# Second mixer of an encoder layer: the two parts of a tile's sums are added before the turn, on GpSimd

## The chip, the cores and the metric

One core of one Trainium2 chip. The metric is the device time of one execution, in microseconds (us), of a kernel that computes one whole encoder layer for 2048 tokens. Engines are named as the profile names them: PE is TensorE, DVE is VectorE, ACT is ScalarE, POOL is GpSimd, SP is SyncE, which here issues the DMAs.

## The reference, cut to what matters

The layer has an input projection, two attention mixers side by side, an output projection, an MLP and a gated extra input. The change is in mixer B only: eight heads of 64 columns, three dilated window patterns over the same keys, a relative-position bias, and a softmax merged over the patterns by its denominators.

```python
def dilated_pattern(q, k, v, rel_bias, window, dilation):
    ...
    sc = jnp.einsum('brnqhd,brnkhd->brnqhk', qs, ks) * (HEAD_DIM ** -0.5)
    sc = jnp.where(valid, sc + bias, NEG_BIG)
    mx = jnp.max(sc, axis=-1)
    e = jnp.exp(sc - mx[..., None])
    den = jnp.sum(e, axis=-1)
    o = jnp.einsum('brnqhk,brnkhd->brnqhd', e, vs) / den[..., None]
    ...
def mixer_b(q, k, v, rel_bias):
    ...
    y = (w[0][..., None] * outs[0] + w[1][..., None] * outs[1] + w[2][..., None] * outs[2]) / w_sum[..., None]
```

For a query tile this comes to: scores, bias, one maximum, one exponential with its sum, the product with the values, and a division by the sum of exponentials.

## The kernel before, in words

The program runs four stages one after the other: the input projection, mixer A, mixer B (`mixer_b_phase`), and the feed stage with everything after the mixers. Mixer B lasts from about 1228 to 1650 us of the span.

Mixer B has 8 heads of 16 query tiles of 128 tokens. Every engine runs the same nest: a hardware loop of four turns, two heads written out in each (`par`), and in each head 16 tiles `n` written out. `N` is the tile's number over all heads. A tile has seven or eight blocks of 128 keys: seven where `n % 4` is 0 or 3 (an edge tile, `first_tile`), eight else (a full tile). All operands of matmuls are split in a high part and a low part, to keep float32's precision with a faster matmul format: queries, keys and values by GpSimd one head ahead, the exponentials inside the tile by ScalarE (high) and VectorE (low).

A tile goes through these steps. TensorE `scores` (L1292, L1300) writes a score tile; VectorE `add_bias` (L1441, three parts) adds the bias and takes maxima, then the row's maximum (L1444). ScalarE `exponential` (L1374) works in SBUF and sums. TensorE `turn` (L1311) transposes seven or eight blocks into two PSUM banks; ScalarE `turned_hi` (L1381, one copy a bank) and VectorE `turned_lo` (L1451) write the high and the low part `pT`. TensorE `values` (L1323) multiplies by the values: stationary are the values' high and low part side by side (64 + 64 columns), moving are both parts of `pT` (256 columns), so that the result `out_acc` holds 128 rows (value part, column) by 256 columns (part of the exponential, query). ScalarE `sums_out` (L1387) copies it to `oT`. TensorE `fold_out` (L1331) transposes both 128-column halves of `oT` back into `out_acc`. VectorE `output` (L1463) multiplies 256 columns by the reciprocal of the sum (`rden`, from `sums_of_two`, L1458) into `y_part`. GpSimd `summed` adds, for two tiles at once, first the two halves of the exponential's parts (L1250) and then the two parts of the values (L1255) into the staging buffer `y_st`, which SyncE stores four tiles at a time (`store`, L1145).

The order on each engine is written out by hand, and each engine takes its instructions strictly in that order. In step `N`:

- TensorE: `scores(N + 2)`, `turn(N + 1)`, `fold_out` of tile `N - 1`, `values(N)`. `values(N)` waits until `output` of tile `N - 2` has freed the accumulator.
- ScalarE: `turned_hi(N + 1)` (two copies), `exponential(N + 2)`, `sums_out(N)`.
- VectorE: `add_bias(N + 2)`, `output` of tile `N - 1`, in even tiles `sums_of_two`, `turned_lo(N + 1)`.
- GpSimd, per head, in long pieces: the last sums of the head before, then eight pieces of the next head's queries and keys (`split_pre`, L1228 with L1232 or L1235, 512 columns each), with `summed` after every second; then all of the next head's values at once (`split_values`, L1240 and L1242, 2048 elements a row), `summed`, then twenty copies of bias tables (`tables`, L1201 to L1214), and two more `summed`.
- SyncE, per head: the stores of chunk 0 and 1, `load_next` (key and query loads, L89, once the split of the head before it in these buffers is done; then the values, one transfer L94 and 24 small ones L102, once `split_values` is done), then the stores of chunk 2 and 3, then the bias tables (L109, L115).

The staging buffer has two halves, so the first `summed` of a head (tiles 0 and 1) waits until the store of the previous head's chunk 2 has landed, and the third until that of chunk 3 has.

```python
def one(h, par, nxt):
    store(h, 0)
    store(h, 1)
    load_next(h + 1, nxt)
    store(h, 2)
    store(h, 3)
    next_tables(h + 1, 1 - par, nxt)
```

## Time and profile before

| what | us |
|---|---|
| median of 3 runs | 3468.54 (3468.3 to 3469.4) |
| the profiled execution, its own time | 3470.07 |
| its span | 3468.3 |
| TensorE busy over the span | 3341.7 |
| VectorE busy | 2360.2 |
| ScalarE busy | 1853.6 |
| GpSimd busy | 1863.4 |
| mean granted clock of TensorE | 0.987 of full |

The profile is of one execution. Its span begins with the first and ends with the last instruction; the execution's own time, 1.8 us longer, holds what lies around it. Busy times are per engine and overlap. A row of the timeline gives the start of a group of neighbouring instructions, its length, engine, line, operation, output<-inputs, shape and count; a bracket behind it gives idle time just before and what ended it. Ends of matmuls are modelled, so starts are the safer reading. "SPq" rows are DMA issues on SyncE's queue; the time of a transfer itself, from issue to landing, stands in the groups of DMAs.

### The profile page before, as it was taken

The page shows a single profiled execution, that of the slowest core. Times are in us where ns is not written, and L with a number is a line of the kernel's source. Part 1 is how long each engine was busy: PE and PEld are TensorE (multiplying, and loading weights), DVE is VectorE, ACT ScalarE, POOL GpSimd, SP SyncE. Part 2 cuts the span into 40 slices and gives each one's busy share as a digit, 9 for nine tenths or more (in the row PEclk, how much of TensorE's full clock was granted, in tenths as well). Part 3 has the DMA queues.
Part 4 walks back from the last instruction along what each step waited for, and adds up shares of the span by engine and source line. Part 5 has one row for each costly group of instructions (what it writes and reads, how often), then busy time and mean ns, then how long its engine had stood idle before and what let it go on. Part 6 is the DMA issues. An engine that isn't in the chain of part 4 may idle for free.

```text
span 3468.3 us, 54646 instructions
## 1 busy us (share of the span) xinstructions
PE 3341.7 (96%) x17366; PEld 2799.6 (81%) x17366; DVE 2360.2 (68%) x4253; ACT 1853.6 (53%) x3489; POOL 1863.4 (54%) x1365
## 2 busy tenths in 40 slices
PE   8999989999999979999799999999999999999997
PEld 6878878888888868888588888888888888888886
DVE  5556679999898989999455574555655556555554
ACT  3222268888888867777434454343544435443333
POOL 5555534445442257667177750777506776067770
PEclk9999999999999989999899999999999999999998
DMA  5455444444442234343444447444474444744443
GB/s 186 159 181 166 143 133 142 147 161 161 153 153 69 47 86 95 83 105 94 165 128 154 150 159 248 158 152 149 154 267 141 151 154 144 256 160 144 144 136 137
DMA packets 234386, 512.87 MB, mean 148 GB/s; under 512 B 113780, under 2 KB 132668, under 8 KB 214364
## 3 DMA queue, kind: packets, MB, share of 16 engines
q1 hardware_dynamic: 224860, 496.91, 44.4%
q10 hardware_dynamic: 9344, 13.73, 1.1%
q8 instruction: 90, 1.47, 0.2%
q14 instruction: 92, 0.75, 0.1%
HBM read 427.43 MB, written 95.58 MB: 151 GB/s over the span
## 4 chain that ended last, share of the span: by engine, by line
PE 47%; DVE 2%; DMA 1%; ACT 1%; issue 1%; POOL 0%; SPq 0%; DVEq 0%
PE feed_bank L1771 45%; PE feed_bank L1854 1%; PE feed_bank L1762 1%; PE feed_bank L1881 1%; ACT feed_xT L1973 0%; DMA feed_w_split<-scr_wG 0%; DMA feed_comb<-scr_wG 0%; POOL feed_w_split L1727 0%; DMA feed_y_in<-scr_yB 0%; DVE feed_xT L2129 0%; DVE feed_sums L2265 0%; DVE feed_total L2219 0%; ACT feed_w_split L2025 0%; DVE feed_total L2144 0%; DVE feed_ms L2108 0%
## 5 line engine op out<-in xcount | busy, mean ns | idle before, releaser
L1727 POOL TENSOR_TENSOR feed_w_split<-feed_w_raw,feed_w_split 128x1024 fp32r<-128x1024 f32 x352 | 882.0, 2515 | 249.6 <-ACT feed_w_split L2025 236.2
L1771 PE MATMUL feed_bank<-feed_w_split,feed_comb 128*128 128x512 f32 x3552 | 822.1, 391 | 16.6 <-DVE feed_sums L2265 7.8
L1771 PEld LDWEIGHTS feed_bank<-feed_w_split,feed_comb 128*128 128x128 f32 x3552 | 664.6, 188 | 162.5 <-POOL feed_w_split L1727 11.6
L1771 PE MATMUL feed_bank<-feed_xT,feed_w_split 128*128 128x512 f32 x3072 | 701.8, 390 | 2.6 <-DVE feed_xT L2129 2.6
L1771 PEld LDWEIGHTS feed_bank<-feed_xT,feed_w_split 128*128 128x128 f32 x3072 | 578.4, 188 | 123.6 <-DVE feed_xT L2129 3.0
L1052 DVE TENSOR_TENSOR mixa_pT<-mixa_turned,mixa_pT 128x512 fp32r<-128x512 f32 x512 | 350.8, 685 | 62.1 <-ACT mixa_pT L994 52.6
L1724 POOL TENSOR_SCALAR feed_w_split<-feed_w_raw 128x1024 fp32r<-128x1024 f32 x128 | 136.5, 1066 | 464.3 <-PE feed_bank L1771 190.1
L994 ACT ACTIVATE mixa_pT<-mixa_turned 128x512 fp32r<-128x512 f32 x512 | 306.7, 599 | 122.6 <-PE mixa_turned L930 103.1
L875 PE MATMUL mixa_out_acc<-mixa_pT,mixa_v_hl 128*128 128x512 f32 x1028 | 365.1, 437 | 0.7 <-DVE mixa_pT L1052 0.7
L2219 DVE TENSOR_TENSOR feed_total<-feed_total,feed_bank 128x512 f32<-128x512 f32 x352 | 224.4, 681 | 195.8 <-PE feed_bank L1771 192.9
L2040 ACT ACTIVATE feed_rl<-feed_bank 128x512 f32<-128x512 f32 x128 | 76.5, 598 | 524.4 <-PE feed_bank L1771 524.4
L2025 ACT ACTIVATE feed_w_split<-feed_w_raw 128x1024 fp32r<-128x1024 f32 x224 | 236.0, 1062 | 189.3 <-PE feed_bank L1771 185.5
L1019 DVE TENSOR_REDUCE mixa_nmax<-mixa_score 128x1 f32<-128x1024 f32 x264 | 322.4, 1221 | 8.4 <-PE mixa_score L862 1.3
L930 PE MATMUL mixa_turned<-layer_ident,mixa_prob 128*128 128x128 f32 x2048 | 306.7, 272 | 0.0
L930 PEld LDWEIGHTS mixa_turned<-layer_ident,mixa_prob 128*128 128x128 f32 x2048 | 252.4, 141 | 55.6
L964 ACT ACTIVATE mixa_prob<-mixa_score,mixa_nmax 128x1024 f32<-128x1024 f32 x263 | 294.3, 1119 | 2.8 <-DVE mixa_nmax L1019 2.8
L862 PE MATMUL mixa_score<-mixa_kT,mixa_qT 128*128 128x512 f32 x1056 | 288.4, 395 | 2.4 <-ACT mixa_prob L964 2.2
L2188 DVE TENSOR_TENSOR feed_comb<-feed_rl,feed_comb 128x256 fp32r<-128x256 f32 x128 | 154.4, 1207 | 175.1 <-ACT feed_comb L2044 174.8
L862 PEld LDWEIGHTS mixa_score<-mixa_kT,mixa_qT 128*128 128x128 f32 x1056 | 198.0, 188 | 50.6 <-ACT mixa_prob L964 4.0
L386 PE MATMUL proj_bank<-proj_w_split,proj_xT 128*128 128x512 f32 (+1 forms) x768 | 180.5, 355 | 0.0
L1381 ACT ACTIVATE mixb_pT<-mixb_turned 128x512 fp32r<-128x512 f32 (+1 forms) x258 | 137.3, 570 | 68.9 <-PE mixb_turned L1311 68.9
L339 POOL TENSOR_SCALAR proj_w_split<-proj_w_raw 128x2048 fp32r<-128x2048 f32 x36 | 73.3, 2036 | 185.9 <-ACT proj_st L453 63.7
(204 smaller groups left out, 5563.1 us busy)
## 6 DMA issues: line engine op xcount, KB each, us to landing
feed_w_raw<-scr_wT SPq DMA_DIRECT2D x160, 512.0 KB, 3.3
feed_w_split<-scr_wG SPq DMA_DIRECT2D x68, 1024.0 KB, 5.0
feed_w_raw<-w_tail_dram SPq DMA_DIRECT2D x128, 512.0 KB, 3.5
proj_w_raw<-w_in_dram SPq DMA_DIRECT2D x39, 1024.0 KB, 5.3
feed_w_raw<-w_ff_dram SPq DMA_DIRECT2D x64, 512.0 KB, 3.5
scr_table<-scr_bias SPq DMA_DIRECT2D x8, 1520.0 KB, 8.6
proj_x_t<-x_dram SPq DMA_DIRECT2D x20, 512.0 KB, 5.9
mixa_queries<-scr_qA SPq DMA_DIRECT2D x36, 256.0 KB, 4.0
```

The lines of the kernel that those rows point to most:

```text
L386: mm = pe.matmul(acc[t][:, 0:width], xT[u][a][:, k0 + kk, t * P:(t + 1) * P], w[m][:, kk, :], start=begin, stop=end)
L862: mm = pe.matmul(score[:, at * BANK:(at + 1) * BANK], qT[g][:, h, :], kT[g][part][:, kc * BANK:(kc + 1) * BANK], start=part == 0, stop=par ...
L875: mm = pe.matmul(out_acc[half][:], v_hl[:, s, g, :], pT[part][:, s % NR, :], start=s % (NT // 2) == 0 and part == 0, stop=s % (NT // 2) == ...
L930: mm = pe.transpose(turned[s % 2][:, h * P:(h + 1) * P], prob[w][:, h, s * P:(s + 1) * P], ident[:])
L964: act.activation(prob[par][:, h, half * 2 * BANK:(half + 1) * 2 * BANK], score[:, 2 * (c % 2) * BANK:2 * (c % 2 + 1) * BANK], ACT.Exp, bia ...
L994: act.activation(pT[0][:, s % NR, :], turned[s % 2][:], ACT.Copy).then_inc(hi_done, 1)
L1019: ve.tensor_reduce(nmax[:, par, c // G, c % G:c % G + 1], score[:, 2 * (c % 2) * BANK: 2 * (c % 2 + 1) * BANK], AXX, ALU.max, negate=True) ...
L1052: ve.tensor_tensor(pT[1][:, s % NR, :], turned[s % 2][:], pT[0][:, s % NR, :].bitcast(F32), ALU.subtract).then_inc(lo_done, 1)
L1727: pool.tensor_tensor(w_sp[slot][:, 1, :], w_raw[:, slot, :], w_sp[slot][:, 0, :].bitcast(F32), ALU.subtract).then_inc(w_lo, 1)
L1771: mm = pe.matmul(dst, lhs, rhs, start=start, stop=stop)
L2025: act.activation(w_sp[slot][:, 0, :], w_raw[:, slot, :], ACT.Copy).then_inc(w_hi_ff, 1)
L2219: ve.tensor_tensor(at, at, acc[2 * (n % 2) + t][:], ALU.add if sign > 0 else ALU.subtract).then_inc(ev_dve, 1)
```

## The change

Four things, all in `mixer_b_phase`:

1. GpSimd's new `halves` adds the two 128-column halves of `oT` into `o_sum`, for every tile. `fold_out` turns `o_sum` once (128 columns) in place of two halves of `oT`, and waits for GpSimd (`sum_done`), no longer for ScalarE. On TensorE it moves behind `values` of the same step.
2. `output` moves from VectorE to ScalarE, at the end of its step: a copy of 128 columns with `rden` as scale. It waits for `fold_done`, and in odd tiles also for `y_ready` and `rden_done`. `y_part` halves in size, and `summed` makes one add per two tiles in place of two.
3. GpSimd's other work is cut into one small piece per tile, each after the tile's `halves`: tiles 0 to 7 take a piece of keys (first) or queries, tiles 8 to 10 the bias tables in three parts, tiles 11 to 14 a quarter each of the values. `summed` follows the piece in even tiles.
4. The waits are renumbered; TensorE waits for the values' split before the first `values` of a head and no longer two tiles before its end. SyncE's order is the same, and so is what each of its items waits for.

```diff
             def load_next(h, nxt):
                 sp.wait_ge(pre_lo, h * PRE + PRE)
                 heads.load_qk(sp, nxt)
-                sp.wait_ge(v_lo, h + 1)
+                sp.wait_ge(v_lo, h * V_PARTS + V_PARTS)
                 heads.load_v(sp, nxt)
...
+            def halves(N, n):
+
+                pool.wait_ge(o_done, N + 1)
+                pool.sem_inc(step, 1)
+                pool.tensor_tensor(o_sum[:, n % 2, :], oT[:, n % 2, 0:P], oT[:, n % 2, P:2 * P], ALU.add
+                                   ).then_inc(sum_done, 1)
 
             def summed(h, e):
 
-                pool.wait_ge(y_done, h * NU + (2 * e + 4))
-                pool.sem_inc(step, 1)
-                both = y_part[:, e % 2, :, :]
-                pool.tensor_tensor(both[:, :, 0:P], both[:, :, 0:P], both[:, :, P:2 * P], ALU.add).then_inc(y_ready, 1)
-                pool.wait_ge(y_ready, h * 16 + (2 * e + 4))
+                pool.wait_ge(y_done, h * NU + (2 * e + 5))
                 if e % 2 == 0:
                     pool.wait_ge(y_out[e // 2 % 2], h * 32 + (e // 4 * 16 + 16))
                 pool.sem_inc(step, 1)
+                both = y_part[:, e % 2, :, :]
                 pool.tensor_tensor(y_st[:, e // 2 % 2, e % 2 * 2:e % 2 * 2 + 2, :], both[:, :, 0:HD], both[:, :, HD:P],
                                    ALU.add).then_inc(y_ready, 1)
 
             with pool.Fori(0, NHB // 2) as it:
                 for par in range(2):
                     h = it * 2 + par
-                    summed(h - 1, 7)
-                    for m in range(PRE):
-                        split_pre(h + 1, 1 - par, m)
-                        if m % 2 == 1:
-                            summed(h, m // 2)
-                    split_values(h + 1, 1 - par)
-                    summed(h, 4)
-                    pool.wait_ge(t_dma, h * 32 + 64)
-                    pool.wait_ge(add_done, h * (3 * NU) + 6)
-                    pool.sem_inc(step, 1)
-                    tables(1 - par)
-                    summed(h, 5)
-                    summed(h, 6)
+                    for n in range(NU):
+                        halves(h * NU + n, n)
+                        if n < PRE:
+                            split_pre(h + 1, 1 - par, (n + 4) % PRE)
+                        elif n == PRE:
+                            pool.wait_ge(t_dma, h * 32 + 64)
+                            pool.wait_ge(add_done, h * (3 * NU) + 6)
+                            pool.sem_inc(step, 1)
+                            other_tables(1 - par)
+                            end_tables(1 - par, (0,))
+                        elif n == PRE + 1:
+                            end_tables(1 - par, (1, 2))
+                        elif n == PRE + 2:
+                            end_tables(1 - par, (3,))
+                        elif n < PRE + 3 + V_PARTS:
+                            split_values(h + 1, 1 - par, n - (PRE + 3))
+                        if n == 0:
+                            summed(h - 1, 7)
+                        elif n % 2 == 0:
+                            summed(h, n // 2 - 1)
...
             def fold_out(count, n):
 
-                pe.wait_ge(o_done, count)
-                for part in range(2):
-                    mm = pe.transpose(out_acc[n % 2][:, part * P:(part + 1) * P], oT[:, n % 2, part * P:(part + 1) * P],
-                                      ident[:])
-                mm.then_inc(fold_done, 1)
+                pe.wait_ge(sum_done, count)
+                pe.transpose(out_acc[n % 2][:, 0:P], o_sum[:, n % 2, :], ident[:]).then_inc(fold_done, 1)
...
                         turn(N + 1, (n + 1) % NU)
+                        values(N, h, par, n)
                         fold_out(N + 1, n - 1)
-                        values(N, h, par, n)
...
+            def output(count, n):
+
+                act.wait_ge(fold_done, count)
+                act.activation(y_part[:, n // 2 % 2, n % 2, :], out_acc[n % 2][:, 0:P], ACT.Copy,
+                               scale=rden[:, n % SLOTS:n % SLOTS + 1]).then_inc(y_done, 1)
...
                         turned_hi(N + 1, n + 1)
                         exponential(N + 2, n + 2)
                         sums_out(N, n)
+                        if n % 2 == 1:
+                            act.wait_ge(y_ready, h * 8 + (n // 2 + 1))
+                            act.wait_ge(rden_done, h * 8 + (n // 2 + 2))
+                        output(N + 1, (n - 1) % NU)
```

## Rows read from the trace of the kernel before

**Rows 1.** The page, busy time of each engine, share of the span, instructions

```profile
PE 3341.7 (96%) x17366; PEld 2799.6 (81%) x17366; DVE 2360.2 (68%) x4253; ACT 1853.6 (53%) x3489; POOL 1863.4 (54%) x1365
```

**Rows 2.** Busy time in one window: us, then busy (count) by engine

```profile
core 0: us, PE busy (x) PEld busy (x) DVE busy (x) ACT busy (x) POOL busy (x), PEclk, DMA share, GB/s
...
1580.00:1630.00 50.00, 48.77 (x362) 43.79 (x361) 49.00 (x176) 40.32 (x82) 35.84 (x55) 1.00 0.56 145
```

**Rows 3.** TensorE in order of time: start, us, engine, line

```profile
1413.01 1.09 PE L1311 MATMUL mixb_turned<-layer_ident,mixb_prob 128*128 128x128 f32 x8
...
1413.93 0.38 PE L1331 MATMUL mixb_out_acc<-layer_ident,mixb_oT 128*128 128x128 f32 x2
...
1414.07 1.20 PE L1323 MATMUL mixb_out_acc<-mixb_pT,mixb_v_hl 128*128 128x256 f32 x8
...
1415.94 1.00 PE L1311 MATMUL mixb_turned<-layer_ident,mixb_prob 128*128 128x128 f32 x7
...
1425.28 1.09 PE L1311 MATMUL mixb_turned<-layer_ident,mixb_prob 128*128 128x128 f32 x8
```

**Rows 4.** ScalarE in order of time, the same stretch

```profile
1411.63 1.16 ACT L1374 ACTIVATE mixb_prob<-mixb_prob,mixb_nmax 128x1024 f32<-128x1024 f32 x1
...
1412.77 0.38 ACT L1387 ACTIVATE mixb_oT<-mixb_out_acc 128x256 f32<-128x256 f32 x1
...
1413.70 1.09 ACT L1381 ACTIVATE mixb_pT<-mixb_turned 128x512 fp32r<-128x512 f32 x2 [0.55 <-PE mixb_turned L1311]
...
1414.67 1.05 ACT L1374 ACTIVATE mixb_prob<-mixb_prob,mixb_nmax 128x896 f32<-128x896 f32 x1
...
1417.77 1.05 ACT L1374 ACTIVATE mixb_prob<-mixb_prob,mixb_nmax 128x896 f32<-128x896 f32 x1 [0.19 <-DVE mixb_nmax L1444]
```

**Rows 5.** VectorE in order of time, where it waited for scores

```profile
1404.05 0.56 DVE L1441 CUSTOM_DVE_ANT_0 mixb_prob<-mixb_score,mixb_t_own 128x384 f32<-128x384 f32 x1 [0.17 <-PE mixb_score L1300]
```

**Rows 6.** Groups by line and shape: count, busy, mean ns, idle before

```profile
L1463 DVE TENSOR_SCALAR mixb_y_part<-mixb_out_acc,mixb_rden 128x256 f32<-128x256 f32 x125 | 60.0, 480 | 0.0
...
L1250 POOL TENSOR_TENSOR mixb_y_part<-mixb_y_part 128x256 f32<-128x256 f32 x63 | 46.5, 737 | 99.7 <-DVE mixb_y_part L1463 99.2 <-POOL mixb_qT L1232 0.5
...
L1255 POOL TENSOR_TENSOR mixb_y_st<-mixb_y_part 128x128 f32<-128x128 f32 x63 | 28.8, 457 | 12.9 <-POOL mixb_y_part L1250 12.9
```

**Rows 7.** GpSimd in order of time, at the first head and a later one

```profile
1254.10 0.62 POOL L1228 TENSOR_SCALAR mixb_qT<-mixb_q_in 128x512 fp32r<-128x512 f32 x1 [3.29 <-DMA mixb_q_in<-scr_qBT]
...
1451.62 0.46 POOL L1255 TENSOR_TENSOR mixb_y_st<-mixb_y_part 128x128 f32<-128x128 f32 x1 [0.18 <-POOL mixb_y_part L1250]
...
1452.04 0.62 POOL L1228 TENSOR_SCALAR mixb_qT<-mixb_q_in 128x512 fp32r<-128x512 f32 x1
...
1454.24 0.62 POOL L1228 TENSOR_SCALAR mixb_qT<-mixb_q_in 128x512 fp32r<-128x512 f32 x1 [0.20 <-POOL mixb_qT L1232]
```

**Rows 8.** SyncE's queue in order of time; a DMA group: KB, us to landing

```profile
1164.22 0.66 SPq L94 DMA_DIRECT2D mixb_v_in<-scr_vB  x1
...
1164.92 13.40 SPq L102 DMA_DIRECT2D mixb_v_in<-scr_vB  x24
...
1283.01 0.41 SPq L94 DMA_DIRECT2D mixb_v_in<-scr_vB  x1
...
1483.29 0.40 SPq L94 DMA_DIRECT2D mixb_v_in<-scr_vB  x1
...
1483.87 16.29 SPq L102 DMA_DIRECT2D mixb_v_in<-scr_vB  x24
...
1500.41 1.12 SPq L1145 DMA_DIRECT2D scr_yB<-mixb_y_st  x2
...
scr_yB<-mixb_y_st SPq DMA_DIRECT2D x32, 128.0 KB, 2.0
```

**Rows 9.** TensorE after an idle stretch, and a window (granted clock third from last)

```profile
1350.29 1.09 PE L1311 MATMUL mixb_turned<-layer_ident,mixb_prob 128*128 128x128 f32 x8 [1.98 <-ACT mixb_prob L1374]
...
1354.80 0.93 PE L1311 MATMUL mixb_turned<-layer_ident,mixb_prob 128*128 128x128 f32 x7
...
1352.00:1353.00 1.00, 1.00 (x6) 1.00 (x6) 1.00 (x3) 1.00 (x3) 0.81 (x1) 0.50 0.72 138
```

More of the change, by code:

```diff
@@ L1098, in mixer_b_phase @@
         oT = k.sb("oT", [P, 2, 2 * P])
-        y_part = k.sb("y_part", [P, 2, 2, 2 * P])
+        o_sum = k.sb("o_sum", [P, 2, P])
+        y_part = k.sb("y_part", [P, 2, 2, P])
         y_st = k.sb("y_st", [P, 2, 4, HD])
@@ L1112, in mixer_b_phase @@
         t_done, hi_done, lo_done, pv_done = (k.sem(n) for n in ("t_done", "hi_done", "lo_done", "pv_done"))
-        o_done, fold_done, y_done = (k.sem(n) for n in ("o_done", "fold_done", "y_done"))
-        y_ready = k.sem("y_ready")
+        o_done, sum_done, fold_done, y_done = (k.sem(n) for n in ("o_done", "sum_done", "fold_done", "y_done"))
+        rden_done, y_ready = k.sem("rden_done"), k.sem("y_ready")
         y_out = k.sems("y_out", 2)
@@ L1118, in mixer_b_phase @@
         PRE = 8
+        V_PARTS = 4
         FIRST_ORDER = (4, 0, 5, 6, 7, 1, 2, 3)
@@ L1202, in tables, with end_tables @@
                                      ).then_inc(t_done_pool, 1)
+            def end_tables(par, residues):
+                near = t_near[:].rearrange("p (v n) -> p v n", v=7)
                 sided = lambda e, r: t_end[par][:, e, r, PAD:P - PAD].rearrange("p (x s n) -> p x s n", s=2, n=PAD)
-                for r in range(RES):
+                for r in residues:
                     for x, z in ((0, r), (r + 1, RES)):
@@ L1217, in _ @@
             pool.wait_ge(t_dma, 32)
-            tables(0)
+            other_tables(0)
+            end_tables(0, range(RES))
             def split_pre(h, par, m):
-                if m == 0:
+                if m == 4:
                     pool.wait_ge(qk_dma, h * (16 * QK_DMAS) + 16 * QK_DMAS)
@@ L1320, in values @@
                 pe.wait_ge(lo_done, N * 2 + 2)
-                pe.wait_ge(y_done, N + 1)
+                pe.wait_ge(y_done, N + 2)
+                if n == 0:
+                    pe.wait_ge(v_lo, h * V_PARTS + V_PARTS)
                 for c, vt in enumerate(tiles, c0):
@@ L1403, in _ @@
                         sums_out(N, n)
+                        if n % 2 == 1:
+                            act.wait_ge(y_ready, h * 8 + (n // 2 + 1))
+                            act.wait_ge(rden_done, h * 8 + (n // 2 + 2))
+                        output(N + 1, (n - 1) % NU)
+            output(NHB * NU + 1, NU - 1)
         @block.vector
@@ L1417, in value_lo @@
             def value_lo(h, par):
[L1418 removed]
+                ve.wait_ge(v_hi, h * V_PARTS + V_PARTS)
                 ve.tensor_tensor(v_hl[par][:, :, HD:2 * HD], v_in[:], v_hl[par][:, :, 0:HD].bitcast(F32), ALU.subtract
[L1420 removed]
+                                 ).then_inc(v_lo, V_PARTS)
             def add_bias(N, par, n):
@@ L1457, in sums_of_two @@
                 ve.wait_ge(exp_done, N + 1)
-                ve.reciprocal(rden[:, at], den[:, at])
-            def output(count, n):
-                ve.wait_ge(fold_done, count)
-                ve.tensor_scalar(y_part[:, n // 2 % 2, n % 2, :], out_acc[n % 2][:, 0:2 * P],
-                                 rden[:, n % SLOTS:n % SLOTS + 1], None, ALU.mult).then_inc(y_done, 1)
+                ve.reciprocal(rden[:, at], den[:, at]).then_inc(rden_done, 1)
             for n in range(6):
@@ L1486, in _ @@
                             add_bias(N + 2, 1 - par, n + 2 - NU)
-                        if n % 2 == 1:
-                            ve.wait_ge(y_ready, h * 16 + (n // 2 * 2 + 1))
-                        output(N + 1, (n - 1) % NU)
                         if n % 2 == 0:
@@ L1492, in _ @@
                         turned_lo(N + 1, n + 1)
-            output(NHB * NU + 1, NU - 1)
 def feed_phase(nc, x, w_ff2, w_tail, pT_d, scr, out, step, ident, feed):
```

35 lines of the change are left out of this document (17 added, 18 removed).

## The prediction

> **What bounds the kernel now.** The page's busy times [rows 1] put TensorE at 96% of the span, but that mixes stages, so I read the second mixer alone, by a window inside it [rows 2]. There the fullest engine is VectorE, 49.0 of 50 us, with TensorE at 48.8, ScalarE 40.3 and GpSimd 35.8. So VectorE looks like the bound, and its group "output", L1463 [rows 6], takes 0.48 us of each tile. The timelines say something else. Four tiles take 1425.28 - 1413.01 = 12.27 us [rows 3], 3.06 a tile. ScalarE goes from one exponential to the next in 1414.67 - 1411.63 = 3.04 us without waiting for VectorE [rows 4]: exponential, then it waits 0.55 us for the turn that this exponential released, two copies, next exponential. That is a ring of latencies between ScalarE and TensorE. In an edge tile (n mod 4 = 0 or 3, seven blocks) the exponential at 1417.77 waited 0.19 us for the row maxima [rows 4], and the maxima come after scores for which VectorE itself waits at times, here 0.17 us [rows 5]. Those scores stand on TensorE behind turn, fold and values. So two rings of waits carry the pitch, and VectorE is full but only partly in them.
>
> **What the change removes on the path.** VectorE loses 0.48 us a tile (61 us over 128). TensorE loses one of two turns: the pair takes 1414.07 - 1413.93 = 0.14 us to issue [rows 3], so 0.07 is saved. In the full tiles the ring exponential, turn, copies stays at 3.04. Its nearest edge value is the 3.04 less a block of exponential (0.10), of turn (0.12) and of copy, about 2.82 if nothing else came last, a mean of 2.93 over both kinds. But there the scores still come last, 0.07 earlier: 3.06 becomes about 3.0. I take 3.02, bounds 2.93 and 3.10.
>
> **What it adds to ScalarE.** 128 scalings of 128 columns out of PSUM. The nearest is the 256-column copy L1387 at 0.38 us [rows 4]; bounds 0.1 and 0.38, taken 0.25. From the start of that copy to the next one stand 1413.70 - 1412.77 = 0.93 us, 0.55 of them idle, and the turn that it needs has been issued before. I cost it at nothing; were the idle time gone, it would be 0.25 a tile, 32 us in all.
>
> **What it adds to GpSimd.** Per head, 8 pairs of adds (0.74 + 0.46) [rows 6] become 24 adds of 0.46 (the new one has L1255's size): 9.6 against 11.0 us, little. The position is new. TensorE's fold of tile n waits for GpSimd's add. From the end of the copy (1413.15) to the fold's new place behind values (about 1415.0, from the values' 1414.07 start) is 1.8 us; less add and semaphore, GpSimd may be 1.2 us late. Next I lay out GpSimd's pieces: an add holds it 0.42 from 1451.62 to 1452.04 [rows 7], a query piece 2.20 [rows 7], a key piece without the last self-wait 2.0, a quarter of the values (512 elements a row too) 2.0. With a sum every second tile the worst pairs take 5.7 us against 6.04: GpSimd keeps up, barely.
>
> **What moves: the values' split, and behind it SyncE's queue.** SyncE loads the values of the head after next only when the split is over, and it issues that head's last two stores after those 25 transfers. The split now ends with tile 14; before it ended two thirds into the head. A quiet instance of this load holds the queue 1164.92 + 13.40 - 1164.22 = 14.1 us; one behind key and query loads 1483.87 + 16.29 - 1483.29 = 16.9 [rows 8]. In the changed kernel those loads have long landed, so I take 14.1 plus 0.5 for the slower heads (bounds 14.1 and 17). These transfers are 16 KB each and cost about 0.5 us of queue, whatever they move.
> The Trainium skill, "DMA: Bandwidth & Descriptors", section "Anatomy of one DMA", counts dispatch at 50 ns and calls descriptor generation small, so that many can be emitted cheaply. By that the queue would be free after some 2 us and there would be no wait in the next paragraph; the rows above speak against it for this load.
>
> **The new wait.** GpSimd's first sum of the next head (n = 2) writes the buffer whose store is that late one. Call V the end of the split.
> - Store landed: V + 0.2 + 14.6 + 0.25 (the gap before the store at 1500.41) + 2.0 (its landing) = V + 17.05 [rows 8].
> - GpSimd would get there at: from tile 14's add, 4 pitches (12.1), its add and piece (2.4), less 2.5 to V: V + 12.0 (13.9 where the loop turns).
> So GpSimd stands about 5 us (3 at a loop turn) in each of heads 1 to 7, and behind it tile 3's add, the fold, ScalarE's output, its copies and all the rest; 1.2 us of slack absorbs a part.
> The head's period follows from this closed chain. From store landed to the next V: sum 0.42; then tile 3's add and its semaphore 0.6, fold 0.07 and scores 0.83 to 1.1 (what turn to turn of 2.93 leaves after 0.92, 0.14 and 1.04 [rows 3]), together 1.6, turn to copy 0.69 [rows 3, 4], copies 0.97, exponential 1.1, copy 0.38, 4.75 to tile 5's add; nine tiles at 3.02 = 27.2; hand-over 0.1; add and last quarter 2.4. Sum 34.85. Period 17.05 + 34.85 = 51.9 us against (1483.29 - 1283.01) / 4 = 50.07 now [rows 8]. Without the wait it would be 16 x 3.02 plus 0.95 for the loop turn = 49.3; the 1.9 us of a loop turn, every second head, I take from the idle time in rows 9.
>
> **The sum.** In head 0 GpSimd's add of tile 1 now stands behind a key piece that waits for a load until 1254.10 [rows 7]; it starts near 1256.5, tile 3's follows 4.75 later, tile 14's after 11 x 3.02, so V is 1297.0 in head 0. Seven periods: 1660.3. Then tile 15's add, fold, scaling and last sum: 2.6. The stage ends at 1662.9. Before, its last sum began a little after 1648.3 and its last store went out at 1648.8; so +14.1 us.
> The clock comes on top. After 1.98 us idle TensorE was granted 0.50, the lower of its levels (1.2 GHz against 2.4), and turn to turn took 4.51 us instead of 2.93 [rows 9, 3]: 1.5 us. In the changed kernel TensorE idles some 3.8 us in four heads, and in three about 1.9 twice; I count three such falls more than now, +4.6. In sum +18.7, taken as 18.5. Against the profiled execution's 3470.1 (span 3468.3) that is 3488.6; it lies 1.5 above the median of the runs, so the forecast is 3487.0.
> Edits costed at nothing: the small pieces themselves (the same work), the finer counts of the semaphores, the later waits for the values' split on TensorE. Their cover is the same slack on GpSimd.
>
> **Rivals.**
> - *No wait on SyncE, the ring shortens.* The stage ends earlier, the mirror of my forecast. If the pitch fell to 2.93 and the store never came last, a period is 47.8: 1296 + 334.6 + 2.6 = 1633.3, -15.5 us, 3453. For it: VectorE at 98%. Against it: the queue's rows and the 3.04 ring. It decides where the load's issue falls below about 10 us. Chance 0.09.
> - *The wait is there but little is left of it, or the change is off the path altogether.* Pitch 3.02 and a store that comes last by a hair: 49.3 x 7, -4.6; or a load at its quick end and no falls of the clock: +5 to +7. So 3464 to 3475. Chance 0.12. 0.2% of this kernel, 7 us, is about what a measurement can tell from no change.
> - *Heavier than forecast.* The clock falls after every wait (+6 more), the load's issue stays near 17 (+2.4 a head, +17), or ScalarE's idle time is too short in edge tiles for scaling and three waits (0.1 in half of the tiles after the wait, +5). Each alone lies in my range, two together make about 3506. Chance 0.15.
> The Trainium skill, "TensorE: Matmul & The Clock Gate", section "HAM oscillation", says that such idle gaps are paid for again at every turn of a loop. By that the first of these would hold: seven falls in place of three. Rows 9 agree that an idle gap can bring the fall; how many of the new gaps would, no row of the kernel before shows.
> That leaves 0.64 for the forecast itself, 3476 to 3500.
>
> **Range and chances.** 3464 to 3506 leaves out the first rival and the far end of the last, under 2 in 10. Faster by over 0.2%: 0.09; within 0.2%: 0.12; slower: 0.79.
>
> **What would show it.** In the profile after: SyncE's late store issued some 15 us after the values' split ends; GpSimd's L1255 counterpart idle for a store, 3 to 5 us, seven times; head periods near 52 us; VectorE down to about 2.5 us busy a tile, with waits for scores; exponentials of full tiles 3.04 us apart in the undisturbed half of a head; ScalarE busier by 0.25 a tile with less idle before its copies; the feed stage unchanged, only later. Wrong it would be if GpSimd's sum in tile 2 waits for no store, if the period is under 50, or if the pitch of undisturbed tiles is under 2.9.

## The result, and the profile after

The changed kernel is slower by 0.3%. Seven runs have a median of 3480.45 us (3475.65 to 3484.7), seven runs of the kernel before, taken beside them, 3468.54; the ratio is 1.003 with an interval of 1.002 to 1.004. The profiled execution is one of the slower ones: its own time is 3484.7, its span 3482.9. Against the profiled execution before (3470.1) that is +14.6, against the medians +11.9. The forecast was 3487.0, with 3464 to 3506 as its range.

Below, the pitch is the time from one tile to the next, and a head's period the time from one of its loads or splits to the same one of the next head. The page of the profile has nothing to tell of where the time went; its sums are those of [rows 1] but for 44 us less on VectorE and 35 more on ScalarE, to which the scaling moved, and 19 more on GpSimd:

```profile
PE 3339.2 (96%) x17237; PEld 2794.1 (80%) x17237; DVE 2316.4 (67%) x4124; ACT 1888.9 (54%) x3618; POOL 1882.2 (54%) x1476
```

SyncE's queue at the edge between the third and fourth head, as in [rows 8]: the values' load, whose start is the end of the values' split, then the 24 small transfers, then the stores of the head, then the next head's load.

```profile
1405.80 0.40 SPq L94 DMA_DIRECT2D mixb_v_in<-scr_vB  x1
1406.39 11.97 SPq L102 DMA_DIRECT2D mixb_v_in<-scr_vB  x24
1418.61 1.07 SPq L1147 DMA_DIRECT2D scr_yB<-mixb_y_st  x2
...
1456.00 0.40 SPq L94 DMA_DIRECT2D mixb_v_in<-scr_vB  x1
```

The load begins at 1405.80 and holds the queue to 1418.36, 12.6 us, and only then the two stores go out. From one such load to the next are 50.2 us here; over six heads, from 1300.64 to 1610.46, 51.6 each (50.0 in the kernel before). GpSimd at the same place, in order of time:

```profile
1415.39 0.46 POOL L1260 TENSOR_TENSOR mixb_o_sum<-mixb_oT 128x128 f32<-128x128 f32 x1 [0.60 <-ACT mixb_oT L1406]
1415.82 0.62 POOL L1237 TENSOR_SCALAR mixb_kT<-mixb_k_in 128x512 fp32r<-128x512 f32 x1
...
1420.84 0.45 POOL L1270 TENSOR_TENSOR mixb_y_st<-mixb_y_part 128x128 f32<-128x128 f32 x1 [3.02 <-DMA scr_yB<-mixb_y_st]
1421.25 0.45 POOL L1260 TENSOR_TENSOR mixb_o_sum<-mixb_oT 128x128 f32<-128x128 f32 x1
1421.67 0.62 POOL L1237 TENSOR_SCALAR mixb_kT<-mixb_k_in 128x512 fp32r<-128x512 f32 x1
...
1423.62 0.46 POOL L1260 TENSOR_TENSOR mixb_o_sum<-mixb_oT 128x128 f32<-128x128 f32 x1
```

The add of tile 2 starts at 1415.39, its key piece follows to 1417.82, and then GpSimd stands 3.02 us for a store. The next add (L1260, for tile 3) could have started some 2.8 us earlier (one pitch of 3.02 behind the last one's 1415.39). TensorE's turns ahead of it, as [rows 3] were, and the fold behind it (L1354, now a single one):

```profile
1381.89 1.09 PE L1333 MATMUL mixb_turned<-layer_ident,mixb_prob 128*128 128x128 f32 x8 [0.30 <-ACT mixb_prob L1393]
...
1393.98 1.09 PE L1333 MATMUL mixb_turned<-layer_ident,mixb_prob 128*128 128x128 f32 x8 [0.35 <-ACT mixb_prob L1393]
...
1421.76 0.33 PE L1354 MATMUL mixb_out_acc<-layer_ident,mixb_o_sum 128*128 128x128 f32 x1 [1.59 <-POOL mixb_o_sum L1260]
```

In the undisturbed part four tiles take 1393.98 - 1381.89 = 12.09 us, 3.02 a tile, where the forecast had 3.02 and the kernel before had 3.06. At 1421.76 the fold has waited for GpSimd. ScalarE in the undisturbed part, as [rows 4]:

```profile
1395.64 1.15 ACT L1393 ACTIVATE mixb_prob<-mixb_prob,mixb_nmax 128x1024 f32<-128x1024 f32 x1
...
1396.78 0.38 ACT L1406 ACTIVATE mixb_oT<-mixb_out_acc 128x256 f32<-128x256 f32 x1
1397.04 0.38 ACT L1411 ACTIVATE mixb_y_part<-mixb_out_acc,mixb_rden 128x128 f32<-128x128 f32 x1
1397.70 1.09 ACT L1400 ACTIVATE mixb_pT<-mixb_turned 128x512 fp32r<-128x512 f32 x2 [0.28 <-PE mixb_turned L1333]
1398.68 1.05 ACT L1393 ACTIVATE mixb_prob<-mixb_prob,mixb_nmax 128x896 f32<-128x896 f32 x1
```

The reader should see two things. Exponential to exponential is still 1398.68 - 1395.64 = 3.04 us. And the new scaling (L1411) sits between the copy of the sums and the copies of the turned blocks: idle time there fell from 0.55 to 0.28 us, and the scaling takes 0.38, not the 0.25 that I put down. The groups by line have it in 120 tiles, and beside it the new add with the idle time before it:

```profile
L1260 POOL TENSOR_TENSOR mixb_o_sum<-mixb_oT 128x128 f32<-128x128 f32 x120 | 55.1, 459 | 79.7 <-ACT mixb_oT L1406 77.9 <-POOL mixb_qT L1241 0.6
...
L1411 ACT ACTIVATE mixb_y_part<-mixb_out_acc,mixb_rden 128x128 f32<-128x128 f32 x120 | 43.9, 366 | 7.9 <-PE mixb_out_acc L1354 7.9
```

The waits of the stage, who waited for whom, us in total, times, longest:

```profile
POOL mixb_y_st L1270 <- DMA scr_yB<-mixb_y_st: 13.6, 4, 4.7
PEld mixb_out_acc L1354 <- POOL mixb_o_sum L1260: 13.1, 5, 4.3
...
ACT mixb_y_part L1411 <- PE mixb_out_acc L1354: 7.9, 5, 3.4
DVE mixb_prob L1471 <- issue: 6.3, 3, 2.1
```

There are four waits for a store, not seven. They come in heads 1, 3, 5 and 7 (counted from 0), in the middle of a turn of the hardware loop. Where the loop turns (before heads 2, 4, 6), VectorE first loses 2.1 us to its own instruction issue (the last row), and GpSimd arrives just when the store has landed. TensorE's clock, by the granted clock of windows (the third value from the right):

```profile
core 0: us, PE busy (x) PEld busy (x) DVE busy (x) ACT busy (x) POOL busy (x), PEclk, DMA share, GB/s
...
1310.00:1320.00 10.00, 6.51 (x43) 5.96 (x44) 5.45 (x19) 5.95 (x14) 4.96 (x7) 0.91 0.44 108
...
1360.00:1370.00 10.00, 9.73 (x66) 9.03 (x65) 7.11 (x25) 8.20 (x18) 7.37 (x10) 0.87 0.27 56
...
1420.00:1430.00 10.00, 8.24 (x65) 7.83 (x64) 7.09 (x24) 7.84 (x19) 8.45 (x13) 1.00 0.48 134
...
1460.00:1470.00 10.00, 8.47 (x55) 8.13 (x56) 7.50 (x25) 7.82 (x18) 5.84 (x9) 0.83 0.16 33
...
1560.00:1570.00 10.00, 8.08 (x52) 7.67 (x51) 6.75 (x25) 6.64 (x14) 4.48 (x7) 0.83 0.37 79
```

TensorE stood still for 3.23 us until 1318.21 and for 1.98, 1.94 and 1.92 us at the loop turns (until 1359.17, 1461.39 and 1563.95), and was granted the lower level, 1.2 GHz in place of 2.4, behind each of these four. The other three stops, 1.59 us until 1421.76, 1.96 until 1524.34 and 1.12 until 1626.07, were followed by no fall. The kernel before stood 1.98, 1.93 and 1.94 us at its loop turns, and only the first was followed by a fall (0.83 in 1350 to 1360, 1.00 in the windows behind the other two). The Trainium skill, "TensorE: Matmul & The Clock Gate", section "HAM oscillation", would have the price paid at every turn; the trace of the changed kernel agrees for its three loop turns and not for the other three stops, and that of the kernel before agrees for one turn of three. The last thing to see is the stage's start. GpSimd in the first head, to be held against [rows 7]:

```profile
1249.05 0.46 POOL L1260 TENSOR_TENSOR mixb_o_sum<-mixb_oT 128x128 f32<-128x128 f32 x1 [11.80 <-ACT mixb_oT L1406]
1254.87 0.62 POOL L1237 TENSOR_SCALAR mixb_kT<-mixb_k_in 128x512 fp32r<-128x512 f32 x1 [5.37 <-DMA mixb_q_in<-scr_qBT]
...
1257.21 0.46 POOL L1260 TENSOR_TENSOR mixb_o_sum<-mixb_oT 128x128 f32<-128x128 f32 x1
```

The add of tile 0 is early, but the piece behind it waits 5.37 us for its load (3.29 before), and the add of tile 1 with it. The ninth transposition (`turn`) of the stage comes 3.8 us later than before, counted from GpSimd's last clearing of a buffer.

### The profile page after: what moved, and what is told of

Same layout as the page of the kernel before. It is cut to its first block, busy times and chain, and to the rows that moved or that the text cites. A ratio compares the mean times of both kernels' runs of the same rounds, so it can differ in the third digit from the quotient of the medians.

```text
span 3482.9 us, 54752 instructions
## 1 busy us (share of the span) xinstructions
PE 3339.2 (96%) x17237; PEld 2794.1 (80%) x17237; DVE 2316.4 (67%) x4124; ACT 1888.9 (54%) x3618; POOL 1882.2 (54%) x1476
## 4 chain that ended last, share of the span: by engine, by line
PE 47%; DVE 2%; DMA 1%; ACT 1%; issue 1%; POOL 0%; SPq 0%; DVEq 0%
PE feed_bank L1791 44%; PE feed_bank L1874 1%; PE feed_bank L1782 1%; PE feed_bank L1901 1%; DMA feed_w_split<-scr_wG 0%; ACT feed_xT L1993 0%; DMA feed_comb<-scr_wG 0%; POOL feed_w_split L1747 0%; DMA feed_y_in<-scr_yB 0%; DVE feed_xT L2149 0%; DVE feed_sums L2285 0%; DVE feed_total L2239 0%; ACT feed_w_split L2045 0%; DVE feed_total L2164 0%; DVE feed_ms L2128 0%
## 5 line engine op out<-in xcount | busy, mean ns | idle before, releaser
L930 PEld LDWEIGHTS mixa_turned<-layer_ident,mixa_prob 128*128 128x128 f32 x2048 | 252.4, 141 | 55.7
L342 POOL TENSOR_TENSOR proj_w_split<-proj_w_raw,proj_w_split 128x2048 fp32r<-128x2048 f32 x36 | 166.2, 4616 | 3.0
```

The costliest lines, as they stand in the source:

```text
L930: mm = pe.transpose(turned[s % 2][:, h * P:(h + 1) * P], prob[w][:, h, s * P:(s + 1) * P], ident[:])
```

## The experiments

All times are medians of several runs, each set beside runs of the kernel before on the same chip: 3471.1 (21 runs) for e1 to e4, 3470.6 (29) for e5 to e8, 3470.8 (14) for e9 to e11. The ratio is to these. The three groups ran on three chips, so a difference between two groups is also one of chips; their kernels before differ by 0.5 us. The diffs show the lines that carry an edit; a "..." stands for lines left out.

**e1: the store goes ahead of the values' load.** The edit to the changed kernel:

```diff
...
                 load_next(h + 1, nxt)
                 store(h, 2)
+                load_values(h + 1, nxt)
                 store(h, 3)
...
```

`load_next` now loads keys and queries only, `load_values` waits for the split and loads the values.

> The changed kernel, with one edit on SyncE: the store of a head's third chunk is issued before the load of the next but one head's values, not after it. Theory Q (the late split of the values holds a store in SyncE's queue, and GpSimd, with the fold behind it, waits for that store): GpSimd waits for no store, head periods fall from 51.6 us to 49.3 (16 tiles of 3.02 and half a loop turn), and the time to about 3464, 4 to 5 below the kernel before. Rival theory H (the hop over GpSimd and the scaling on ScalarE lengthen the tile itself): periods stay near 51.6, the time within 3 of the changed kernel's 3480. Theory C (the granted clock, lowered after idle stretches, is most of the loss): about half of the gain of Q, 3470 to 3474, as the falls at the loop turns stay.

Measured: 3470.6, ratio 0.9997 (0.9988 to 1.0006). The wait for stores is gone, and with it 9.9 us of the medians, 11 by the ratios. Theory Q holds in kind: one place in SyncE's order carries the loss against the kernel before. Its size does not. The loads, head by head:

```profile
1400.22 0.40 SPq L94 DMA_DIRECT2D mixb_v_in<-scr_vB  x1
...
1448.69 0.40 SPq L94 DMA_DIRECT2D mixb_v_in<-scr_vB  x1
...
1499.47 0.40 SPq L94 DMA_DIRECT2D mixb_v_in<-scr_vB  x1
```

A head without a loop turn takes 48.47 to 48.49 us as forecast (16 x 3.03), but those with one 52.05, 50.78 and 50.43, so 49.8 on average, not 49.3. The first head's split ends only 1.0 us earlier than in the changed kernel (the load behind it goes out at 1299.68 against 1300.64). e1 is level with the kernel before, not 5 us better. In GpSimd's row of tile 2's sum no wait is left:

```profile
1412.19 0.45 POOL L1274 TENSOR_TENSOR mixb_y_st<-mixb_y_part 128x128 f32<-128x128 f32 x1
```

**e2: the same stall removed from the other side.** The values' quarters move to tiles 8 to 11, the tables to 12 and 13.

```diff
...
-                        elif n == PRE:
+                        elif n < PRE + V_PARTS:
+                            split_values(h + 1, 1 - par, n - PRE)
+                        elif n == PRE + V_PARTS:
...
```

> The changed kernel, with one edit on GpSimd: the four quarters of the values' split stand at tiles 8 to 11, and the bias tables at tiles 12 and 13. SyncE's order is the changed kernel's. The split ends 3 tiles (9 us) earlier, so the stores behind the load come 9 us earlier too. Theory Q: no wait for a store is left, time 3464 as in e1, within 2. Theory H: near 3480. If it were something in e1's order of transfers itself, e1 and e2 would part by more than 3 us.

Measured: 3499.9, ratio 1.0080 (1.0066 to 1.0094). The expectation fails by 36 us. No wait for a store is left here either, but another took its place, in the list of waits:

```profile
DVE mixb_prob L1469 <- POOL mixb_t_end L1221: 25.6, 7, 3.7
```

VectorE needs the next head's tables for the first two tiles of that head, whose bias it adds in tiles 14 and 15. Copied in tiles 12 and 13 they come 3.7 us late in each of seven heads. So the late place of the values' split had a reason: the two kinds of pieces have different due times, and the split is the one that can be late, as long as nothing that somebody waits for stands behind it on SyncE. As a second proof of the store's wait e2 is of no use: it takes one wait away and brings another.

**e3: the late split alone, in the kernel before.**

```diff
-                    split_values(h + 1, 1 - par)
                     summed(h, 4)
...
                     summed(h, 5)
+                    split_values(h + 1, 1 - par)
                     summed(h, 6)
```

> The kernel before, with the suspected cause alone: the values' split, in one piece, moved behind the bias tables, between the sums of tiles 10, 11 and 12, 13. It then ends near tile 15, as late as in the changed kernel or later. Theory Q: GpSimd waits some 4 to 8 us for a store in each of seven heads. In this kernel nothing of the tile's own chain goes through GpSimd; only VectorE's output waits for a free part buffer, two tiles later, so I expect the loss to be smaller than the wait: head periods of 50 to 53, time 3470 to 3490. Theory H: no more than 2 us above the kernel before, 3470.

Measured: 3529.6, ratio 1.0164 (1.015 to 1.0178). Slower than any theory had it, and by another wait, which I had overlooked:

```profile
PE mixb_score L1292 <- POOL mixb_v_hl L1242: 33.7, 7, 4.8
```

In the kernel before TensorE waits for the values' split two tiles before a head's end. The seven waits are 34 of the 58 us lost; behind each of them the granted clock also falls (to 0.66 to 0.88 in the lowest window of 10 us), and how much of the other 24 us that is no run separates. The change had moved that wait to the head's first product; part 4 of the change, which I had costed at nothing, is what allows a split that ends with tile 14. The run says nothing on the stores; e6 repeats it with that wait moved.

**e4: control, e1's order in the kernel before.** The same edit on SyncE as e1's.

> Control: the kernel before with e1's edit on SyncE alone. In the kernel before the store has landed some 3 us before GpSimd wants its buffer. Theory Q: no change, 3468.5 within 2. If this order of transfers gains by itself, by less contention of transfers for instance, it shows here, and e1 would have to be read against it.

Measured: 3470.2, ratio 1.0000 (0.9991 to 1.0009). As expected: the order of transfers alone gains nothing where nobody waits for the store, so e1's gain is the wait's.

**e5: the scaling back on VectorE.**

```diff
-                        output(N + 1, (n - 1) % NU)
...
                         turned_lo(N + 1, n + 1)
+                        output(N + 1, (n - 1) % NU)
```

The first line is the end of ScalarE's step, the last that of VectorE's, there as a multiplication of 128 columns.

> e1 (the changed kernel with the store ahead of the values' load) with one part of the change undone: the scaling of the turned tile goes back to VectorE, 128 columns in place of 256, at the end of VectorE's step. It tells what the move to ScalarE is worth. Ring theory (the pitch of full tiles is set by exponential, turn, copies, exponential): the pitch of full tiles stays at 3.03 to 3.04 though VectorE is busier by about 0.36 a tile and ScalarE idle again by as much; time within 2 us of e1. Rival theory V (VectorE's full queue set the pitch before and its relief made the 3.02): the pitch goes back to 3.06, 16 x 8 x 0.04 = 5 us more than e1.

Measured: 3468.3, ratio 0.9996 (0.9987 to 1.0005), against e1's 0.9997; the medians, of two chips, are 2.3 us apart. One window of e5, then the same of e1, busy by engine:

```profile
1580.00:1630.00 50.00, 48.00 (x347) 42.31 (x345) 47.94 (x175) 40.85 (x84) 38.35 (x77) 1.00 0.57 155
```

```profile
1580.00:1630.00 50.00, 48.01 (x348) 42.29 (x348) 43.65 (x156) 44.91 (x101) 38.02 (x72) 1.00 0.58 156
```

VectorE is 47.9 of 50 us busy in the one and 43.7 in the other, ScalarE 40.9 and 44.9, and four tiles take 12.08 to 12.17 us in both, with the same four distances (3.04, 2.92, 2.96 and 3.17). Moving the scaling bought nothing at this order of work. In e5 VectorE scales 128 columns and not the 256 of the kernel before, so for that kernel's fuller VectorE it is e11 that tells.

**e6: the late split alone, now with TensorE's wait moved.** e3 with

```diff
                             if n == NU - 2:
                                 pe.wait_ge(pre_lo, h * PRE + 2 * PRE)
-                                pe.wait_ge(v_lo, h + 2)
...
                 pe.wait_ge(y_done, N + 1)
+                if n == 0:
+                    pe.wait_ge(v_lo, h + 1)
```

> The kernel before with the late split of the values as in e3, and TensorE's wait for that split moved from two tiles before a head's end to the head's first product with the values, as the changed kernel has it. e3 hit that wait: TensorE stood 4.8 us for the split in each of seven heads, so it did not show the store's wait alone. Theory Q: now the store's wait shows, GpSimd stands some 3 to 8 us for a store in most heads, and since only the part buffers hang on it in this kernel (VectorE's output, two tiles later), the time is between the kernel before and e3, 3475 to 3500. If the split itself lying late costs nothing without a wait: 3471.

Measured: 3479.2, ratio 1.0022 (1.0013 to 1.0031); one of the twelve runs, 4210.3 us, is left out of the ratio. The kernel before, given only the late split, loses 8.6 us and shows the wait of the changed kernel:

```profile
POOL mixb_y_st L1255 <- DMA scr_yB<-mixb_y_st: 18.6, 4, 6.8
```

Four waits, 18.6 us, the same heads. Less of it reaches the end than in the changed kernel, as expected, since a pair of part buffers lies between GpSimd and the rest. Cause removed (e1) and cause alone (e6) agree.

**e7: GpSimd's pieces one tile later.** e1 with

```diff
...
-                        if n < PRE:
-                            split_pre(h + 1, 1 - par, (n + 4) % PRE)
+                        if 0 < n <= PRE:
+                            split_pre(h + 1, 1 - par, (n + 3) % PRE)
...
```

and the tables in tiles 9 and 10.

> e1 with GpSimd's pieces one tile later: tile 0 of a head has none, tiles 1 to 8 take keys and queries, 9 and 10 the tables, 11 to 14 the values as before. In the first head the piece at tile 0 waits 4.8 us for a load with the adds of tiles 1 and on behind it; up to the ninth turn after the start of the stage e1 is 3.1 us behind the kernel before. Theory S (that start is what eats e1's gain): the start is 2 to 4 us shorter, time 3467 to 3469 against e1's 3470.6. Rival: the wait only moves to tile 1 and nothing changes, within 1 us of e1.

Measured: 3463.2, ratio 0.9979 (0.997 to 0.9987), 7.4 below e1 (6.9 when each is taken against its own kernel before) and the first version faster than the kernel before. The wait for the first load fell from 4.8 to 2.0 us:

```profile
POOL mixb_kT L1241 <- DMA mixb_q_in<-scr_qBT: 2.0, 1, 2.0
```

The stage's whole gain lies in the first head: its ninth turn comes at 1266.63 in place of 1272.60, 6.0 us earlier, and the stage's last sum 6.1 us earlier (1643.31 in place of 1649.42). The two profiled executions are 8.2 us apart; the other 2 us lie behind the stage and are not explained. The adds of the first tiles no longer stand behind the load, and TensorE is at the full clock from 1250 on. Up to that ninth turn, and counted as above, e7 is also 2.7 us quicker than the kernel before.

**e8: scores ahead of the values' product.** e1 with

```diff
...
-                            scores(N + 2, par, n + 2)
...
                         turn(N + 1, (n + 1) % NU)
...
+                            scores(N + 3, par, n + 3)
...
                         values(N, h, par, n)
...
```

The scores of tile 2 are added ahead of the loop.

> e1 with TensorE's order changed: the scores of a tile are issued before the product with the values, not after it, one tile further ahead. It breaks the second ring (turn, values, scores, maxima, exponential) and leaves the first (exponential, turn, copies, exponential; 3.04 in a full tile, about 2.82 in an edge tile, mean 2.93). Two-ring theory: exponentials wait for no maxima in undisturbed tiles, the pitch falls from 3.02 to 2.93 to 2.97, time 5 to 11 us below e1, 3460 to 3465, the first clear gain over the kernel before. Rival theory G (GpSimd's pieces, 5.7 us for two tiles in the first half of a head, or the later values, which ScalarE's copy of the sums waits for, come next): the pitch stays above 3.00, within 3 us of e1.

Measured: 3454.1, ratio 0.9953 (0.994 to 0.9966), 16.5 below e1, more than the 5 to 11 expected. TensorE's turns:

```profile
1380.84 1.09 PE L1337 MATMUL mixb_turned<-layer_ident,mixb_prob 128*128 128x128 f32 x8
...
1383.87 1.09 PE L1337 MATMUL mixb_turned<-layer_ident,mixb_prob 128*128 128x128 f32 x8 [0.20 <-ACT mixb_prob L1398]
...
1386.79 0.98 PE L1337 MATMUL mixb_turned<-layer_ident,mixb_prob 128*128 128x128 f32 x7
...
1389.57 0.96 PE L1337 MATMUL mixb_turned<-layer_ident,mixb_prob 128*128 128x128 f32 x7
...
1392.44 1.09 PE L1337 MATMUL mixb_turned<-layer_ident,mixb_prob 128*128 128x128 f32 x8
```

Four tiles take 1392.44 - 1380.84 = 11.60 us here, 2.90 a tile, and 11.60 to 11.69 in the stretches around: of the four distances from turn to turn 3.03 and 2.92 stay, and e1's 2.96 and 3.17 become 2.78 and 2.87. ScalarE in an edge tile of the same stretch:

```profile
1387.03 0.36 ACT L1416 ACTIVATE mixb_y_part<-mixb_out_acc,mixb_rden 128x128 f32<-128x128 f32 x1
1387.37 1.03 ACT L1405 ACTIVATE mixb_pT<-mixb_turned 128x384 fp32r<-128x384 f32 x2
1388.30 1.04 ACT L1398 ACTIVATE mixb_prob<-mixb_prob,mixb_nmax 128x896 f32<-128x896 f32 x1
...
1389.66 0.39 ACT L1411 ACTIVATE mixb_oT<-mixb_out_acc 128x256 f32<-128x256 f32 x1 [0.24 <-PE mixb_out_acc L1351]
...
1391.07 1.15 ACT L1398 ACTIVATE mixb_prob<-mixb_prob,mixb_nmax 128x1024 f32<-128x1024 f32 x1
```

In undisturbed tiles no exponential waits for maxima any more (4 such waits in the stage against 43 in e1), so the second ring is broken. In full tiles the first ring stays, with turns 3.03 us apart as in e1. In an edge tile, from 1388.30 to 1391.07, the exponentials are 2.77 us apart. That is near the forecast's edge value of 2.82, but not by its ring: the copies wait for no turn there, ScalarE goes from scaling to copies and from copies to exponential without idle time, and its one wait (0.24 us, before the copy of the sums at 1389.66) is for the product with the values. At this pitch it is ScalarE's own step, now longer by the scaling, that is all but full in edge tiles.

**e9: e7 and e8 together.**

> e8 (store ahead of the load, scores ahead of the values' product) and e7 (GpSimd's pieces one tile later) together. e7 gained 7.4 us on e1 and e8 16.5. If they are independent (one shortens the stage's start and the heads' edges, the other the pitch): 3446 to 3449. If GpSimd is now what comes last in the first half of a head (5.7 us of pieces for two tiles of 2.90): 3450 to 3454, with waits of TensorE's fold for GpSimd's add in tiles 2 to 9.

Measured: 3449.1, ratio 0.9937 (0.9923 to 0.9951). The best version, 31 us below the changed kernel and 22 below the kernel before. 5.0 of e7's 7.4 us are left in it, at the upper end of the first expectation; its turns are as far apart as e8's, 11.60 to 11.69 us for four tiles.

**e10: e9 with the scaling on VectorE.** The same edit as e5's.

> e9 with the scaling back on VectorE (128 columns), as e5 did to e1, where it made 2 us less. At a pitch of 3.02 VectorE had room for it. At 2.90 VectorE needs 2.58 and the 0.4 of a scaling, 2.98, more than the pitch: the move to ScalarE should now be worth something, 0.08 a tile or 10 us, so 3455 to 3460. Rival: the two engines are as good as each other here too, within 2 of e9.

Measured: 3483.8, ratio 1.0042 (1.0028 to 1.0055), 35 us above e9, three times what I expected. VectorE's load does not explain that: it is busy 46.6 us in the 50 from 1380 on, less than in e5. Its order explains a part. The longer stops of the stage, then VectorE in order of time:

```profile
DVE mixb_y_part L1485 <- PE mixb_out_acc L1356: 25.4, 61, 2.3
...
DVE mixb_prob L1463 <- issue: 10.3, 3, 3.8
```

```profile
1394.93 0.35 DVE L1485 TENSOR_SCALAR mixb_y_part<-mixb_out_acc,mixb_rden 128x128 f32<-128x128 f32 x1 [0.36 <-PE mixb_out_acc L1356]
1395.29 0.56 DVE L1463 CUSTOM_DVE_ANT_0 mixb_prob<-mixb_score,mixb_t_own 128x384 f32<-128x384 f32 x1
```

The fold is now last on TensorE behind scores and values, and VectorE's scaling waits for it, with the next tile's bias (the row below) behind the scaling, 61 times in the stage. Four tiles take 12.3 to 12.7 us, and a head without a loop turn 49.5 us against e9's 46.6. That is only some 3 us a head. A head with a loop turn takes 55.3 to 55.7 against 48.3 to 49.9, and there, in three heads, lies about two thirds of what the seven periods lose, 18.5 of 27.3 us: VectorE stands up to 3.8 us for its own instruction issue, and then up to 2.3 for the fold. Why the issue takes longer there no run shows. So with scores first the end of VectorE's step is a bad place for the scaling; how much VectorE's load alone would cost there, which was the question, e10 does not tell.

**e11: scores first in the kernel before.**

> The kernel before with e8's order on TensorE alone (turn, fold, scores, values), VectorE's scaling of 256 columns and the two turns in place. Two-ring theory with VectorE's load: the second ring is broken here too, but VectorE is busy 3.06 of 3.06 us a tile, start to start some 2.98, so the pitch can only fall to about 3.0: time 3461 to 3468. If it falls to 2.90 as in e8, VectorE's load was no bound at all and the change has no share in e8's gain: 3452 to 3456. If nothing changes (3470), VectorE was the bound before.

TensorE's wait for the values' split moved with the order, to just ahead of the product in the last tile but one. Measured: 3462.0, ratio 0.9977 (0.9968 to 0.9986). Within the expectation of a full VectorE. One window:

```profile
1580.00:1630.00 50.00, 49.15 (x371) 46.01 (x370) 49.44 (x175) 42.71 (x85) 36.91 (x65) 1.00 0.42 115
```

VectorE is busy 49.4 of 50 us and four tiles take some 11.95, 2.99 each, against 2.90 to 2.92 in e8. Two things follow. The kernel before had the same work on VectorE at a pitch of 3.06, so VectorE, full as it was, was not what set that pitch. And the change has a share in e8, which this order of TensorE alone does not give. That this share is VectorE's relief is argued from the 49.4 of 50 and not shown, since e8 differs from e11 in the whole change (and e10, which was to show it, met another wait).

## Why the prediction was right, point by point

*What bounds the kernel.* Right. "Two rings of waits carry the pitch": e11 (same load on VectorE, ring broken, pitch down by 0.07), e5 (scaling on VectorE or not, same pitch) and e8 (pitch down by 0.12) show it. The pitch was forecast at 3.02 and measured at 3.02, and from the place forecast: the full tiles' distance of 3.04 stays, and one of the others falls from about 3.08 to 2.96.

*The queue on SyncE.* Right in mechanism, off in size, and two errors cancelled. I had the last head's split end at 1660.3, and in the profiled execution it ended at 1660.1. That is luck: the first head's split ended 3.5 us later than I had it (below), and the seven periods behind it took 359.7 us in place of 363.3, although I had counted the falls of the clock on top and the measured periods hold them. I had 17.05 us from the end of the split to the landed store, and it is 15.2 (1420.84 less 1405.65): the load held the queue for 12.6 us in this head and not 14.6. The 14.1 that I started from was itself not quiet: its first small transfer took 2.2 us. The 24 transfers had lain behind the key and query loads in all heads but the quiet one, and in that one behind two loads of 256 KB for mixer A; I had no row for them without such company. With the shorter hold the store comes last only in four heads. At the loop turns GpSimd arrives 15.9 us after the split (1369.52 less 1353.58), not 13.9, since VectorE's issue takes 2.1 us there and TensorE starts again at a lower clock. So of the seven waits forecast four came (4.7, 3.0, 3.4 and 2.6 us, 13.6 together), and the three at loop turns did not.

*What it would be without the wait.* Wrong by 4 to 5 us: forecast -4.6 (my terms give nearer -4.2), measured level (e1, 0.9997). Two terms failed. The heads with a loop turn take 50.4 to 52.1 us and not 50.2, some 3 us over the stage. The other term is head 0. I let tile 1's add start at 1256.5 and the chain run on at full pace; it started at 1257.2, and the stage's first split ended at 1300.5 (1299.5 in e1) and not at 1297.0, since TensorE, which had stood for tile 1's add, was then at the lower clock for a part of the time (0.84 and 0.82 in the windows 1250 to 1270, where the kernel before shows 1.00), for which my sum had no term. e7 mends only this start and comes to 3463, 7.4 below the kernel before. That does not make the -4.6 right after all: it was said of a kernel whose first piece stands where e1 has it.

*The clock.* The forecast counted three more falls, 4.6 us. The windows show four against one, so the count is right for the profiled execution, though outside the loop turns TensorE stood 3.23, 1.59, 1.96 and 1.12 us and not some 3.8 four times. What one costs can be read from heads with a loop turn: with a fall they take 51.9 to 52.1 us (the changed kernel, three times; e1, once), without one 50.4 and 50.8 (e1), so 1.1 to 1.6 us, as taken. The spans of the profiled executions of the changed kernel and of e1, which keeps one fall at its first loop turn, differ by 13.9 us; four waits of 13.6 us together, less 1.2 us of slack each, are 8.8, and three falls of 1.5 are 4.6, together 13.4. But the medians differ by only 9.9 us, and the profiled execution is the slowest of its seven. Which stops bring a fall differs even between equal ones (1.93 and 1.98 us in the kernel before), so the others may have had fewer; they have no trace. For the median run the 4.6 us are therefore not shown; fewer falls there would explain up to that much of the 6.5 us by which 3487.0 is too high.

*ScalarE.* Costed at nothing, rightly at a pitch of 3.02: e5 and e1 are level. Its size was wrong, 0.37 us for 128 columns against my 0.25. From 256 columns (0.37) to 128 the length did not fall at all, so the line through the larger copies was no guide (one of the two has a scale and the other none, so that width alone is not separated).

*GpSimd's adds.* 0.46 us as taken, and its pieces keep up at 3.02. The edits costed at nothing hold, with one exception in the reading: the moved wait of TensorE for the split. It costs nothing because it was moved; e3 shows what it costs where it was, a wait of 4.8 us a head.

Open: why the 24 transfers hold the queue for 11.97 us in one head and 13.57 in another, and how many falls of the clock a median run has.

## What to carry to other kernels

When work is moved later on one engine, follow its completion through every queue that waits for it: here a split that ended some 13 us later in its head (the load behind it goes out 5.4 us before TensorE's first transposition at 1359.17, where in the kernel before it went out 19.1 us before the one at 1350.29) held a DMA queue, behind that a store, behind that a staging buffer, and at the end the matmul engine. An engine that is 98% busy need not be the bound; look for the ring of waits whose length is the pitch, and try the edit that breaks it (here one change of order, worth 16 us in the changed kernel and 9 in the kernel before) before moving load between engines (e5: worth nothing at the old order). And a step that is put into the tile's own chain makes every other wait of its engine a wait of the whole pipeline.

## What the runs showed that I had not expected

A ScalarE copy of 128 columns out of PSUM with a scale takes 0.366 us in the mean, that of 256 columns without one 0.372. VectorE's scaling, by contrast, fell from 0.48 to 0.34 us with half the columns. And 24 transfers of 16 KB hold the queue for 12.0 to 13.6 us, 0.5 us each, with only one load of 512 KB ahead of them: each lands 1.7 us after its issue (the median), while the next goes out 0.5 us behind it, so it is their issue that holds the queue. The Trainium skill, "DMA: Bandwidth & Descriptors", section "Anatomy of one DMA", calls the making of descriptors small, but of DMAs that GpSimd issues; these are issued by SyncE, so the prediction held against them a figure for another path, and no run here issues them from GpSimd.
